# Value rows summed one quarter behind their gathers in place of two

## The reference

```python
q = (hf @ w_pq).reshape(n, PEER_HEADS, 2, PEER_DHALF)
s = jnp.einsum('nhsd,hskd->nhsk', q, sub_keys)
sv, si = lax.top_k(s, PEER_TOPK)                # 16 of 128, twice
...
fv, fp = lax.top_k(cand, PEER_TOPK)             # 16 of 256: 16 experts per head
eidx = ...                                      # 8 heads x 16 = 128 experts per token
u = jnp.take(u_tab, ec, axis=0)                 # a key row of 1024 numbers each
act = jax.nn.gelu(jnp.einsum('cd,ced->ce', hc, u))
wgt = gc * act
vr = jnp.take(v_tab, ec, axis=0)                # a value row of 1024 numbers each
out = jnp.einsum('ce,ced->cd', wgt, vr)         # sum of 128 weighted value rows
```

## Time and profile before

| what | value |
|---|---|
| time, median of 3 runs | 1968.49 us (1967.65 to 1968.7) |
| time of the profiled execution | 1969.88 us |
| its span, first to last instruction | 1967.9 us |
| mean granted PE clock | 0.809 |
| busy: PE, DVE, ACT, POOL | 69%, 64%, 30%, 55% |
| bytes moved | 701.85 MB, mean 357 GB/s |
| of these by POOL's gathers | 545.33 MB |

### The profile page before, as it was taken

The page is one execution under the profiler, slowest core; times in us unless marked ns, Lnnn a source line. Parts: engine busy times, 40 slices in busy tenths (PEclk is TensorE's granted clock), DMA queues, the critical chain, the costliest instruction groups (busy, mean ns, idle before and its releaser), DMA issues.

```text
span 1967.9 us, 23637 instructions
## 1 busy us (share of the span) xinstructions
PE 1350.3 (69%) x7252; PEld 859.3 (44%) x7252; DVE 1257.6 (64%) x3102; ACT 595.9 (30%) x1656; POOL 1083.4 (55%) x1062
## 2 busy tenths in 40 slices
PE   6998999857888778888887876444444443544445
PEld 5887799845656445566555553111110110111111
DVE  3265436477777878778678866666667666666640
ACT  2446424232344345332223432112122112211110
POOL 0100010166666467667655767767677777677764
PEclk9999999979998889989898997565666566765667
DMA  9756345599999999999999999999999999999997
GB/s 368 257 182 211 105 154 200 195 373 409 409 407 360 358 348 378 381 410 409 408 406 389 409 409 401 408 403 401 406 405 404 404 400 406 371 409 409 404 399 301
DMA packets 202445, 701.85 MB, mean 357 GB/s; under 512 B 22568, under 2 KB 32368, under 8 KB 202032
## 3 DMA queue, kind: packets, MB, share of 16 engines
q0 software_dynamic: 149760, 545.33, 70.2%
q1 hardware_dynamic: 52560, 155.02, 21.6%
HBM read 691.26 MB, written 11.06 MB: 357 GB/s over the span
## 4 chain that ended last, share of the span: by engine, by line
DMA 20%; PE 12%; issue 12%; DVE 11%; POOL 10%; ACT 2%; POOLq 0%; DVEq 0%; ACTq 0%; SPq 0%
DMA arena<-in_v_tab,pku 14%; POOL arena L2198 10%; PE y L1171 7%; DMA arena<-in_u_tab,pku 5%; DVE arena L2023 4%; PE acc L807 4%; DVE pku L2044 1%; DVE arena L1753 0%; DVE pk L2043 0%; ACT arena L1264 0%; PE turned L1151 0%; DVE pku L2060 0%; DVE pk L2059 0%; DMA key_rows<-arena 0%; DVE arena L2047 0%
## 5 line engine op out<-in xcount | busy, mean ns | idle before, releaser
L2198 POOL DMA_INDIRECT arena<-in_u_tab,pku x520 | 539.9, 1038 | 352.7 <-issue 153.7
L1171 PE MATMUL y<-arena 128*32 128x512 f32 x2080 | 410.4, 906 | 462.6 <-DMA arena<-in_v_tab,pku 462.6
L2198 POOL DMA_INDIRECT arena<-in_v_tab,pku x520 | 528.5, 1016 | 275.5 <-issue 141.3
L807 PE MATMUL acc<-arena 128*128 128x264 f32 (+1 forms) x2304 | 552.0, 398 | 20.7 <-ACT arena L1280 8.3
L807 PEld LDWEIGHTS acc<-arena 128*128 128x128 f32 x2304 | 449.6, 198 | 123.5 <-issue 49.6
L2023 DVE CUSTOM_DVE_ANT_0 arena<-arena,h_bank 128x1024 f32<-128x1024 f32 x240 | 291.2, 1219 | 252.2 <-DMA arena<-in_u_tab,pku 251.7
L2023 DVE CUSTOM_DVE_ANT_0 arena<-arena 128x1024 f32<-128x1024 f32 x280 | 335.3, 1222 | 92.2 <-DMA arena<-in_u_tab,pku 74.0
L1171 PEld LDWEIGHTS y<-arena 128*32 128x32 f32 x2080 | 82.5, 143 | 704.7 <-issue 690.7
L1507 ACT ACTIVATE pk<-pk 128x1 f32<-128x1 f32 x520 | 103.6, 281 | 2.1
L1529 ACT CAST pku<-turned 128x8 uint32<-128x8 f32 x64 | 10.3, 161 | 309.3 <-PE turned L1151 264.5
L2241 POOL TENSOR_TENSOR o_lo<-arena,o_hi 128x256 fp32r<-128x256 f32 x8 | 6.6, 850 | 156.7 <-ACT o_hi L1383 156.7
(11 more groups left out here) (249 smaller groups left out, 1809.6 us busy)
## 6 DMA issues: line engine op xcount, KB each, us to landing
arena<-w_mod SPq DMA_DIRECT2D x48, 512.0 KB, 5.9
arena<-w_pq SPq DMA_DIRECT2D x32, 512.0 KB, 7.0
arena<-w_xr SPq DMA_DIRECT2D x20, 512.0 KB, 8.4
arena<-w_qk SPq DMA_DIRECT2D x20, 512.0 KB, 7.3
arena<-w_gr SPq DMA_DIRECT2D x20, 512.0 KB, 7.2
arena<-w_rnn SPq DMA_DIRECT2D x16, 640.0 KB, 7.0
arena<-in_u_tab,pku POOLq DMA_INDIRECT x520, 8.4
arena<-in_v_tab,pku POOLq DMA_INDIRECT x520, 7.9
```

The lines of the kernel that those rows point to most:

```text
L807: mm = pe.matmul(a[:, 0:n], w[:, k, :], rhs[:, k, 0:n], start=(k == 0), stop=(k == ks - 1))
L1171: mm = pe.matmul(y[rows, h, :], spread[g % NTURN][:, 32 * j:32 * j + 32], rows_v[j][:, h * 512:(h + 1) * 512], start=first and (g != SAMPL ...
L2198: pool.indirect_dma_start(out=row, out_offset=None, in_=table, in_offset=bass.IndirectOffsetOnAxis(ap=idx, axis=0), **more).then_inc(signa ...
```

## The change

One number: `SUMS_LAG` goes from 2 to 1.

```diff
-DOTS_LAG, NAMES_LEAD, TURN_LEAD, SUMS_LAG = 2, 6, 2, 2
+DOTS_LAG, NAMES_LEAD, TURN_LEAD, SUMS_LAG = 2, 6, 2, 1
```

## The result

The changed kernel takes 1994.25 us (median of 4 runs, 1989.89 to 1996.08), against 1968.6 us for the kernel before beside it: ratio 1.012, 95% interval 1.0107 to 1.0133. It is slower by 1.2%, some 24 us. The forecast was 1966.0 us, so it had the wrong sign. The profiled execution took 1993.97 us (span 1992.0 us, granted clock 0.797).

What follows compares the result with a forecast made beforehand. Transfers were taken as the bound from 800 us on, the dense chain at 600 to 800 us. Terms -2.4 + 1.8 - 2.0 = -2.6 us on the median 1968.49 gave 1965.9, stated as 1966.0 us; forecast band 1961 to 1970, range 1957 to 1980.

Steps and rivals of the forecast that it cites:

- What bounds the kernel: Transfer rate from 800 us to the end; the chain of dense work over PE, ACT and DVE at 600 to 800 us.
- Entry into the stretch, 586 us: At 586 us, a projection and two matmuls move behind a sum's 6.33 us wait; dense work 4.5 us later.
- one quarter, 6.9: Upper bound in us on how late dense work gets at 586 us; the lower bound was 0.
- Inside it: From 590 to 830 us, earlier sums free places and POOL runs ahead by up to 6.9 us; 2.4 us gained.
- falling below half of 50.2: Sign that the forecast is right: POOL's hold-ups from 590 to 830 us, 50.2 us before, fall below half.
- The dots don't wait: At 600 to 800 us DVE's dots never wait for a key row, so POOL running ahead buys no pace.
- 800 to 1130 us: A shorter queue still feeds the transfers; only the hole at 1073 us grows, by 0 to 3.7; 1.8 us lost.
- that sign: Sign of a wrong forecast: rate between 800 and 1075 us below 400 GB/s, meaning the shorter queue does not feed the transfers.
- The sample tile: At 1660 to 1680 us the first sum goes ahead of the weight turn; sum and POOL 2.0 us earlier, 2.0 gained.
- Rival 3: Slower, 1981 us: at 600 to 810 us dense work stands behind landings, key rows holding POOL; chance 0.18.
- its sign of decision: PE's wait for value rows in 600 to 800 us passes some 15 us and DVE starts to wait for PE.
- Rival 4: Slower by the clock, 1977 us: 13 sums at 600 to 800 us take 3.64 for 1.92 us after waits; chance 0.06.

Runs made afterwards that it cites:

- One sum alone: Against the kernel before, only sum 10 (counted from 0, the one at 586 us) stood one quarter earlier, in mid-quarter; 1982.13 us, ratio 1.0056.
- The run of quarters 36 to 69 alone: Against the kernel before, only sums of value rows gathered in quarters 36 to 69 (sums 12 to 28) stood one quarter earlier; 1969.44 us, ratio 0.9992.
- sum 35: Against the kernel before, only this sum (counted from 0, last row gathered in quarter 96) stood one quarter earlier; 1972.71 us, ratio 1.0013.
- the late stretch alone: Against the kernel before, only sums of value rows gathered from quarter 140 on (after about 1215 us) stood one quarter earlier; 1968.97 us, ratio 0.9986.
- at its quarter's end: Against the kernel before, sum 10 alone one quarter earlier, but behind that quarter's last product; 1970.83 us, ratio 1.0005.
- the run of quarters 72 to 139: Against the kernel before, only sums of value rows gathered in quarters 72 to 139 stood one quarter earlier, in mid-quarter; 1979.87 us, ratio 1.0048.

## Why the prediction was wrong, step by step

- *What bounds the kernel* was right from 1215 us on: but for the tile switch nothing moved there. ("No engine is busy for more than four fifths" was a little too strong: by the earlier trace rows PE is busy for 81% from 800 to 1075 us, and DVE for 94% in the 25 us behind that.) For 600 to 800 us "the chain of dense work over PE, ACT and DVE sets the pace" was right too, and should have led to the result: what delays that chain is lost.
- *Entry into the stretch, 586 us* is **the step that failed**. The place, the wait and what moves behind it were all named; the size, "4.5 us later", counted how long the moved matmuls run on PE. What counts is when their readers start. DVE's gate arithmetic began 15.13 us later (580.67 to 595.80): PE came to this place 4.07 us later (the products before it end at 580.24 in place of 576.17; it was 5.0 us late at the turns ahead of them, 566.61 against 561.66, behind the new wait of sum 7), then 6.20 of waiting, 3.57 for the sum and 1.29 for the product. The prediction had nothing for what the sums before 586 us delay. The readers' work, which the wait used to hide, now follows it. The upper bound of "one quarter, 6.9" was no bound. One sum alone: 11 us.
- *Inside it* failed by itself too. That sums held POOL before was right (value rows, 45.9 us), and earlier sums do free the value places (15.6 us now). But POOL did not run ahead: the hold moved to the key places, where gathers wait for dots (46.1 us in place of 3.3), and POOL's hold-ups rose to 62.7 us in place of falling below half of 50.2. "The dots don't wait" says that key rows come early enough, and not that the dots come early enough for the gathers. The run of quarters 36 to 69 alone, in which nothing is late at 586 us, shows the same exchange (value rows 16.8 us, key rows 33.4) and gains 1.6 us (-0.2 to 3.5) where this term had 6.9 for dense work that is not late.
- *800 to 1130 us*: 1.8 us forecast, about 10 measured. The term looked only at the hole after 1073 us; the loss is made between 832 and 1057 us. One part of it is a sum with dense products behind it (sum 35, 2.6 us); the rest is open. The rate did fall below 400 GB/s. What the prediction would read from that sign, a queue too short to feed the transfers, is refuted between 600 and 800 us and open after that.
- *The sample tile* was right in kind: the sum starts 1.9 us earlier (2.0 forecast), POOL goes on 1.1 us earlier (2.0 forecast), and the late stretch alone gains 2.8 us (0.8 to 4.5).
- *Rival 3* named the mechanism (dense work behind landings, key places that hold POOL) and the direction, and gave 1981 us, 13 below the measured time and already outside the stated range, which ended at 1980. Its place was off, as the first loss is made by sums up to 586 us, and so was its sign of decision: PE's wait for value rows fell, and 16.2 us of it in another run cost nothing.
- *Rival 4*, the clock: the profile of the run from quarter 140 on has PE busy for 1362.1 us, 11.8 more than before, and loses nothing; sum 10 took 3.31 us after 7.73 us of waiting at its quarter's end and 3.44 after 8.59 in its middle, and only the second cost time. The price of this rival was misread too: by the earlier trace rows the sum at 617.66 takes 3.40 us without a wait of its own, and three more of the 13 that this rival counts at 1.92 take 3.50 to 3.64; in the changed kernel one such sum takes 3.64 us there, the one at 749.18.

## What to carry to other kernels

In a list that runs in order, price a wait by the readers of what stands behind it, not by the length of the work that moves: ask which engine next needs a product from behind the wait, and whether it used to work during that wait. A total of waits on one engine says little about this; PE's went down here while the kernel lost 24 us. When one constant moves many instructions, look for the few places where a long wait passes a product that starts a chain on other engines: here one of 130 sums, moved ahead of two such matmuls, made almost half of the loss by itself.

## What the runs showed of the hardware

Of two executions with the same list on PE up to that point, one ran 32 small products at little more than half the rate of the other. The window from 835 to 845 us, before and in the run of quarters 72 to 139, whose first moved sum comes only at 857 us:

```profile
835.00:845.00 10.00, 7.88 (x55) 6.12 (x56) 4.97 (x11) 3.43 (x12) 8.17 (x7) 0.88 1.03 408
```

```profile
835.00:845.00 10.00, 9.68 (x45) 6.79 (x45) 0.97 (x4) 1.56 (x8) 7.87 (x8) 0.50 1.02 407
```

The products took 3.75 us at a granted clock of 0.88 (near the upper level, 2.4 GHz) and 7.00 us at 0.50 (the lower one, 1.2 GHz), after a sum that had waited 3.36 us in the one and 3.83 us in the other. "TensorE: Matmul & The Clock Gate" of the Trainium skill (HAM oscillation) says that a wait for transfers can throttle the engine, so that the next burst of matmuls starts at half clock. The trace agrees in the second execution; in the first, after a wait only 0.47 us shorter, the burst ran near the upper level. So a few us of the loss that this one profile shows in that stretch may be the clock's and not the change's.
